# Attention with nine query steps per head instead of ten: the two short query chunks share one step

## The reference, cut to what matters

```
h = rmsnorm(x);  p = h @ w_in                      # uv | c_q | c_kv | k_rope | gate_a | gate_b
A = chunked gating of uv over 128-token chunks, @ w_a_out
q = rmsnorm(rmsnorm(c_q) @ w_uq)   per head: 8 heads, 128 plain + 64 rotary columns
k = rmsnorm(k_nope | k_rope),  v = 128 columns per head
o = softmax(q k^T * scale) @ v                     # bidirectional, within the group
B = o @ w_b_out
x = x + (sigmoid(gate_a) * A + sigmoid(gate_b) * B) @ w_out
x = x + expert-choice SwiGLU of rmsnorm(x): 16 experts, 2*n/16 tokens each
```

## Time and profile before

| what | value |
|---|---|
| median of three runs | 2089.08 us |
| lowest and highest of them | 2088.29 and 2089.18 us |
| span of the profiled execution, first to last instruction | 2087.1 us |
| instructions | 33261 |
| mean granted clock of TensorE | 0.994 |
| busy: TensorE, VectorE, ScalarE, GpSimd | 98%, 65%, 46%, 43% of the span |

### The profile page before, as it was taken

The page is one execution under the profiler, slowest core; times in us unless marked ns, Lnnn a source line. Parts: engine busy times, 40 slices in busy tenths (PEclk is TensorE's granted clock), DMA queues, the critical chain, the costliest instruction groups (busy, mean ns, idle before and its releaser), DMA issues.

```text
span 2087.1 us, 33261 instructions
## 1 busy us (share of the span) xinstructions
PE 2042.8 (98%) x13266; PEld 1683.2 (81%) x13266; DVE 1351.1 (65%) x1629; ACT 951.2 (46%) x1188; POOL 904.8 (43%) x640
## 2 busy tenths in 40 slices
PE   8999999999899999999999999899999999999997
PEld 8888888888789888888888887677777777777775
DVE  7864455456767477777754358876676667766774
ACT  8112211113555366666631032455556555555563
POOL 0975555566655376666642601412222222222221
PEclk9999999999999999999999999899999999999999
DMA  4223544324677622222134432688887778888873
GB/s 156 100 104 133 169 161 149 115 85 134 232 242 246 213 66 84 95 88 66 56 109 156 158 142 81 240 353 313 312 300 284 277 286 313 311 313 312 300 283 106
DMA packets 168938, 398.98 MB, mean 191 GB/s; under 512 B 16513, under 2 KB 88193, under 8 KB 168833
## 3 DMA queue, kind: packets, MB, share of 16 engines
q1 hardware_dynamic: 154096, 344.43, 45.0%
q0 software_dynamic: 7680, 20.98, 4.4%
q10 hardware_dynamic: 7056, 32.12, 4.4%
HBM read 318.19 MB, written 79.30 MB: 190 GB/s over the span
## 4 chain that ended last, share of the span: by engine, by line
PE 85%; DVE 8%; ACT 2%; POOL 2%; issue 1%; DMA 1%; SPq 0%; DVEq 0%; POOLq 0%; ACTq 0%
PE PS L1626 25%; PE PS L419 13%; PE PS L420 13%; PE PS L421 13%; PE PS L1657 8%; PE PS L1411 3%; PE PS L1398 1%; DVE topi L2663 1%; PE PS L1402 1%; PE PS L1399 1%; PE PS L1400 1%; PE PS L1401 1%; PE PS L1339 1%; DVE topv L2661 1%; DVE work L2665 1%
## 5 line engine op out<-in xcount | busy, mean ns | idle before, releaser
L419 PE MATMUL PS<-act_hi,w_hi 128*128 128x256 f32 (+1 forms) x800 | 275.2, 344 | 7.2 <-POOL w_lo L878 3.4
L420 PE MATMUL PS<-act_lo,w_hi 128*128 128x256 f32 (+1 forms) x800 | 270.1, 338 | 0.0
L421 PE MATMUL PS<-act_hi,w_lo 128*128 128x256 f32 (+1 forms) x800 | 269.7, 337 | 0.0
L981 POOL TENSOR_SCALAR prob<-prob,small 128x1024 f32<-128x1024 f32 (+1 forms) x80 | 200.6, 2508 | 120.7 <-DVE small L2551 120.7
L1051 POOL DMA_INDIRECT y_s<-ob_s,ixs_s x16 | 43.8, 2738 | 352.9 <-DVE ob_s L2822 352.9
L419 PEld LDWEIGHTS PS<-act_hi,w_hi 128*128 128x128 f32 x800 | 151.7, 190 | 24.8 <-POOL w_lo L878 3.7
L1626 PE MATMUL PS<-ehi,xT_hi 128*128 128x512 f32 x520 | 165.4, 399 | 0.6 <-DVE xT_lo L2736 0.4
L421 PEld LDWEIGHTS PS<-act_hi,w_lo 128*128 128x128 f32 x800 | 151.5, 189 | 16.3
L420 PEld LDWEIGHTS PS<-act_lo,w_hi 128*128 128x128 f32 x800 | 151.8, 190 | 14.8 <-issue 0.7
L1626 PE MATMUL PS<-elo,xT_hi 128*128 128x512 f32 x520 | 160.6, 390 | 0.0
L1626 PE MATMUL PS<-ehi,xT_lo 128*128 128x512 f32 x520 | 160.5, 390 | 0.0
(11 more groups left out here) (375 smaller groups left out, 5465.6 us busy)
## 6 DMA issues: line engine op xcount, KB each, us to landing
raw<-in_w_gate SPq DMA_DIRECT2D x64, 1024.0 KB, 8.8
raw_more<-in_w_up SPq DMA_DIRECT2D x32, 1024.0 KB, 12.6
raw_w<-in_w_up SPq DMA_DIRECT2D x32, 1024.0 KB, 16.6
w_raw<-in_w_in SPq DMA_DIRECT2D x16, 1024.0 KB, 7.7
w_raw<-in_w_down SPq DMA_DIRECT2D x15, 1024.0 KB, 5.7
stg<-in_w_down SPq DMA_DIRECT2D x15, 1024.0 KB, 7.8
gt<-in_w_down SPq DMA_DIRECT2D x15, 1024.0 KB, 13.0
raw_end<-in_w_down SPq DMA_DIRECT2D x15, 1024.0 KB, 14.9
```

The source lines that it names most:

```text
L419: pe.matmul(out, lh, rh, start=first, stop=False)
L420: pe.matmul(out, lh, rl, start=False, stop=False)
L421: return pe.matmul(out, ll, rh, start=False, stop=last)
L981: pool.tensor_scalar(prob[:, n % 3, 0:kn], prob[:, n % 3, 0:kn], prec[:, s:s + 1], None, ALU.mult).then_inc(S["norm_pool"], 1)
```

## The change

The two sample chunks of a head become one step, step 4 of nine, so there are 72 steps instead of 80. In the double step TensorE computes the scores of both chunks side by side in one bank, VectorE takes both maxima in one reduce and both biases in one operation, ScalarE still makes two exponentials, GpSimd multiplies both by their reciprocals with one operation whose second operand is broadcast. The four transposes go to one bank and are copied out in one operation on each engine, and the six value matmuls follow each other. The pairs of the prompt keep their halves.

The nine pieces of the next head are now turned in steps 1 to 8: none in step 0, one each in steps 1 to 5, pieces 5 and 6 in step 6, pieces 7 and 8 in steps 7 and 8. Piece 5 goes through bank 5, which the double step's transposes leave free, the others through bank 7; the transposes that follow in bank 5 wait for piece 5. SP loads the next tokens at a head's step 0, behind the store of the double step's values, under the same waits as before.

```diff
-ORD = (0, 1, 2, 3, 8, 9, 4, 5, 6, 7)
-STEPS = H * NCH
+TOKENS = ((0,), (1,), (2,), (3,), (8, 9), (4,), (5,), (6,), (7,))
+SH = len(TOKENS)
+STEPS = H * SH
+S_STEP = 4
...
+def turned_at(n):
+
+    h, s = divmod(n, SH)
+    first = PIECES * (h + 1)
+    return () if h == H - 1 else {0: (), S_STEP + 2: (first + 5, first + 6)}.get(s, (first + s - (s < S_STEP + 2),))
+
+
+def pair_of(n):
+
+    h, s = divmod(n, SH)
+    return 5 * h + (s // 2 if s < S_STEP else (s + 1) // 2)
+
+
+def half_of(n):
+
+    s = n % SH
+    return None if s == S_STEP else s % 2 if s < S_STEP else (s + 1) % 2
...
 def returns_at(n):
 
-    k = n - (STEPS - NCH + 2)
-    return {0: 0, 2: 1, 4: 2, 6: 3, 10: 4}.get(k)
+    k = n - (STEPS - SH + 2)
+    return {0: 0, 2: 1, 4: 2, 6: 3, 9: 4}.get(k)
...
         def x_bank(x):
-            return bank(6 + x % 2 if x < PIECES else 7)
+            if x < PIECES:
+                return bank(6 + x % 2)
+            return bank(5 if x % PIECES == 5 else 7)
...
             for n in range(STEPS + 4):
-                h, s = divmod(n, NCH)
-                if n % 2 == 0 and n >= 6:
-                    store_values((n - 6) // 2)
-                if h + 2 < H:
-                    if s == 9:
-                        sp.wait_ge(S["x_pe"], PIECES * (h + 1) + 9)
-                        load_queries(h + 2)
-                        sp.wait_ge(S["v_lo_pool"], h + 2)
-                        load_keys(h + 2)
-                if n == 2 * NCH:
+                h, s = divmod(n, SH)
+                if n >= 5 and half_of(n - 5) != 0:
+                    store_values(pair_of(n - 5))
+                if 0 < h < H - 1:
+                    if s == 0:
+                        sp.wait_ge(S["x_pe"], PIECES * h + 9)
+                        load_queries(h + 1)
+                        sp.wait_ge(S["v_lo_pool"], h + 1)
+                        load_keys(h + 1)
+                if n == 2 * SH:
...
                 pool.wait_ge(S["recip_dve"], n + 1)
-                pool.tensor_scalar(prob[:, n % 3, 0:kn], prob[:, n % 3, 0:kn], prec[:, s:s + 1], None,
-                                   ALU.mult).then_inc(S["norm_pool"], 1)
-                if s == 4 and h + 1 < H:
+                if s == S_STEP:
+                    both = prob[:, n % 3, 0:2 * TS].rearrange("p (c k) -> p c k", c=2)
+                    pool.tensor_tensor(both, both, prec[:, c:c + 2].unsqueeze(2).to_broadcast([P, 2, TS]),
+                                       ALU.mult).then_inc(S["norm_pool"], 1)
+                else:
+                    pool.tensor_scalar(prob[:, n % 3], prob[:, n % 3], prec[:, c:c + 1], None,
+                                       ALU.mult).then_inc(S["norm_pool"], 1)
+                if s == S_STEP and h + 1 < H:
                     split_values(h + 1)
...
-                free = x - 1 if h == 0 else x
+                free = x - 1 if h == 0 or i == 6 else x
...
-                q = slice(c * P, (c + 1) * P)
-                for o in range(0, kn, BANK):
-                    w = min(BANK, kn - o)
-                    out, k = bank(s_bank(n) + o // BANK, w), slice(k0 + o, k0 + o + w)
+                w = min(BANK, kn)
+                for c, o in [(c, o) for c in TOKENS[s] for o in range(0, kn, BANK)]:
+                    q, k = slice(c * P, (c + 1) * P), slice(k0 + o, k0 + o + w)
+                    first = s_bank(n) * BANK + o + c % 2 * w * (s == S_STEP)
+                    out = PS[:, first:first + w]
...
                 pe.wait_ge(S["norm_pool"], n + 1)
                 if n > 0:
                     pe.wait_ge(S["pt_lo_dve"], n)
+                if n % SH == S_STEP + 1 and n < STEPS - SH:
+                    pe.wait_ge(S["x_hi"], turned_at(n + 1)[0] + 1)
+                    pe.wait_ge(S["x_lo"], turned_at(n + 1)[0] + 1)
...
                 if n >= 4:
-                    values((n - 4) // 2, n % 2)
-                if h < H - 1 and s < PIECES:
-                    turn_head(PIECES * (h + 1) + s)
+                    values(n - 4)
+                if n < STEPS:
+                    for x in turned_at(n):
+                        turn_head(x)
...
-                act.activation(prob[:, n % 3, 0:kn], bank(s_bank(n), kn), ACT.Exp, bias=nmx[:, s:s + 1],
-                               scale=rq[:, h, c:c + 1], accum_out=psumr[:, s:s + 1]).then_inc(S["exp_act"], 1)
+                for c in TOKENS[s]:
+                    o = slice(c % 2 * kn, (c % 2 + 1) * kn) if s == S_STEP else slice(0, kn)
+                    last = act.activation(prob[:, n % 3, o], bank(s_bank(n), width(n))[:, o], ACT.Exp, bias=nmx[:, c:c + 1],
+                                          scale=rq[:, h, c:c + 1], accum_out=psumr[:, c:c + 1])
+                last.then_inc(S["exp_act"], 1)
...
-                if n == 0:
-                    high_head(PIECES)
                 if n < STEPS:
                     expo(n)
-                if n % 2 and 5 <= n:
-                    out_pair((n - 5) // 2)
-                if h < H - 1 and s < PIECES and n > 0:
-                    high_head(PIECES * (h + 1) + s)
+                if n >= 4 and half_of(n - 4) != 0:
+                    out_pair(pair_of(n - 4))
+                if n < STEPS:
+                    for x in turned_at(n):
+                        high_head(x)
...
-                dve.tensor_scalar(nmx[:, s:s + 1], mx[:, s:s + 1], rq[:, h, c:c + 1], -1.0, ALU.mult,
-                                  ALU.mult).then_inc(S["bias_dve"], 1)
+                dve.scalar_tensor_tensor(out=nmx[:, c:c + cn], in0=mx[:, c:c + cn], scalar=-1.0, in1=rq[:, h, c:c + cn],
+                                         op0=ALU.mult, op1=ALU.mult).then_inc(S["bias_dve"], 1)
```

More of the change, by code:

```diff
@@ L1381, in scores @@
             def scores(n):
-                h, s = divmod(n, NCH)
-                hd, c = heads[h % 2], ORD[s]
-                k0, kn = keys(c)
+                h, s = divmod(n, SH)
+                hd = heads[h % 2]
+                k0, kn = keys(TOKENS[s][0])
                 if s == 0:
@@ L1405, in turn_prob @@
             def turn_prob(n):
-                kn = keys(ORD[n % NCH])[1]
+                kn = width(n)
                 pe.wait_ge(S["norm_pool"], n + 1)
@@ L1409, in turn_prob, with values @@
                     pe.wait_ge(S["pt_lo_dve"], n)
+                if n % SH == S_STEP + 1 and n < STEPS - SH:
+                    pe.wait_ge(S["x_hi"], turned_at(n + 1)[0] + 1)
+                    pe.wait_ge(S["x_lo"], turned_at(n + 1)[0] + 1)
                 for k in range(kn // P):
-                    last = pe.transpose(bank(4, kn)[:, k * P:(k + 1) * P], prob[:, n % 3, k * P:(k + 1) * P], ident[:])
+                    o = (0, 2, 1, 3)[k] if n % SH == S_STEP else k
+                    last = pe.transpose(bank(4, kn)[:, o * P:(o + 1) * P], prob[:, n % 3, k * P:(k + 1) * P], ident[:])
                 last.then_inc(S["probT_pe"], 1)
-            def values(pr, half):
+            def values(n):
+                pr, half = pair_of(n), half_of(n)
                 h = pr // 5
                 hd = heads[h % 2]
-                k0, kn = keys(ORD[2 * (pr % 5)])
-                ks = kn // P // 2
-                if half == 0:
-                    pe.wait_ge(S["pt_lo_dve"], 2 * pr + 2)
+                k0, kn = keys(first_of(pr))
+                ks = kn // P
+                if half != 1:
+                    pe.wait_ge(S["pt_lo_dve"], n + 1 if half is None else n + 2)
                     if pr % 5 == 0:
@@ L1424, in values @@
                         pe.wait_ge(S["values_act"], pr)
-                for k in range(half * ks, (half + 1) * ks):
+                for k in range(ks) if half is None else range(half * ks // 2, (half + 1) * ks // 2):
                     v = slice(k0 + k * P, k0 + (k + 1) * P)
                     last = mm3(pe, bank(6, 2 * P), hd["v_hi"][:, v], hd["v_lo"][:, v], pt_hi[:, pr % 2, k],
-                               pt_lo[:, pr % 2, k], k == 0, k == 2 * ks - 1)
-                if half:
+                               pt_lo[:, pr % 2, k], k == 0, k == ks - 1)
+                if half != 0:
                     last.then_inc(S["values_pe"], 1)
@@ L2034, in high @@
             def high(n):
[L2035 to L2037 removed]
                 act.wait_ge(S["probT_pe"], n + 1)
[L2039 to L2042 removed]
+                if half_of(n) != 1 and pair_of(n) > 1:
+                    act.wait_ge(S["values_pe"], pair_of(n) - 1)
+                act.activation(turned_part(pt_hi, n), turned_bank(n), ACT.Copy).then_inc(S["pt_hi_act"], 1)
             def expo(n):
[L2045 to L2047 removed]
+                h, s = divmod(n, SH)
+                kn = keys(TOKENS[s][0])[1]
                 act.wait_ge(S["bias_dve"], n + 1)
@@ L2563, in _ @@
                     low(n - 2)
-                if n == 0:
-                    low_head(PIECES)
                 if n < STEPS:
                     inverse(n)
-                if h < H - 1 and s < PIECES and n > 0:
-                    low_head(PIECES * (h + 1) + s)
```

(2 more changed lines are left out.)

49 lines of the change are left out of this document (23 added, 26 removed).

## The result

The changed kernel takes 2130.79 us (median of four runs, 2128.46 to 2131.39) against 2089.13 us: ratio 1.020, 95% interval 1.0187 to 1.0212. It is 41.7 us slower. The forecast was 2102.0 with a range of 2096 to 2115, so the sign was right and the size short by 28.8 us. The profiled execution has a span of 2128.8 us and a mean granted clock of 0.985.

The account below looks back on a forecast made before the run. TensorE, busy 98% of the span, was taken as the bound. Heads 1 to 6 +12.0, head 0 +1.5, head 7 -2.3 and clock +1.7 gave +12.9 on 2089.1: 2102.0 us, range 2095.8 to 2115.

Parts of the forecast that it names:

- TensorE's own work of a head: Nine steps of a head's matmuls and transposes on TensorE: 42.41 us against 43.51, if nothing new waits.
- the gap: TensorE idles before the next head's first scores, waiting for the last piece: 3.1 us, seven times, 21.7 us.
- The loads of the next head: SP's load of the next tokens, issued about 2 us later, was called covered before its first piece: 0.
- the gap is hidden: Rival: the last piece's chain ends before TensorE reaches the next head's scores, so the kernel gets faster, 2078.6 us; 8%.
- what would show it: Signs: seven TensorE idles of about 3 us released by VectorE's L2501, heads of about 45.5 us, head 7 near 39.2.
- I take one such fall among seven gaps, +1.7: Granted clock behind TensorE's idle stretches before a head's scores: one drop to mostly 1.2 GHz, costing 1.7 us.
- the clock falls behind every gap: Rival: the clock drops after all seven idle stretches before a head's scores, 11.9 us instead of 1.7, 2112.2 us; 17%.
- The walk of step 7: Delays counted from the start of step 6: step 7's exponential at 9.28 us, ahead of step 8's start at 9.86.
- The bias in its new form reads a column more: nothing beside 0.21: VectorE's bias operation with its extra column read was taken to add nothing to its 0.21 us.
- 0.9 of slack: Bank 5: piece 5's low part done about 6.3 us, step 7's transposes start at 7.20, so no wait.
- the microsecond that I allowed: Head 0: 40.7 us against 39.27, +1.5, trusted to 1 us.
- The pile-up rival: ScalarE and VectorE lose another 0.6 us in step 6; TensorE's idle becomes 3.7 us, 4.2 more, 2106.2 us; 10%.

Follow-up runs that it names:

- experiment 10: Changed kernel with old bias form for single chunks, own buffer for the double step, last piece in step 7, piece kinds reordered: 2077.41 us, ratio 0.995.
- experiment 3: Changed kernel with the single-chunk bias in its old form and own buffers for the double step's turned probabilities: 2108.87 us, ratio 1.0096.
- experiment 6: Changed kernel with the last piece back in step 7, two pieces in step 6, none in step 8, loads at step 8: 2090.86 us, ratio 1.0012.
- experiment 11: The kernel of experiment 10 without the double step's own buffers: 2081.83 us, ratio 0.9969.
- experiment 12: The kernel of experiment 10 without the own buffers and with the changed kernel's two-tensor-input bias in all steps: 2093.40 us, ratio 1.0024.
- experiment 7: Changed kernel with a head's last piece copied out ahead of the last step's exponential and reciprocal: 2123.16 us, one execution.
- experiment 8: The kernel of experiment 3 with the last piece ahead of exponential and reciprocal, but behind the low half of step 6: 2103.19 us, ratio 1.0069.
- experiment 1: Changed kernel with the single-chunk bias in its old form, the double step keeping the new one: 2126.58 us, ratio 1.018.
- experiment 2: Changed kernel with own buffers for the double step's turned probabilities: 2121.13 us, ratio 1.016.
- experiment 4: Changed kernel with GpSimd splitting the next head's values one step later: 2127.43 us, one execution.

## Why the prediction was right in sign and wrong in size

**What held.** TensorE's own work of a head was right to 0.04 us (42.41; 42.44 in experiment 10), so was the place of the gap, the order that makes it and its length once the two unforeseen waits are gone (3.09 us by pitch, measured 3.19 in experiment 3). GpSimd's broadcast multiply took 1.04 us where I took 1.10. The loads of the next head cost nothing in the changed kernel (they did in experiments 6, 11 and 12, where less time lies between their issue and the first piece). The rival "the gap is hidden" had the price 2078.6; the version that hides it measured 2077.4, though that near match has luck in it, since 1.8 us of its gain lie ahead of attention. In heads 1 to 6 of the changed kernel steps 1 to 5 are each within 0.02 us of the working. Of "what would show it", the gaps' releaser held in substance: the view names ScalarE's L2068 six times of seven, but L2552, as L2501 is called now, ends 0.05 us behind it (807.46 against 807.41) and 0.10 ahead of the scores. Head 7 took 41.3 instead of 39.2, 1.65 of it for the fall in its first step.

**The steps that failed**, with their share of the missing 28.8 us:

- *The clock: "I take one such fall among seven gaps, +1.7".* There were seven, and they cost 15.0 us, 2.1 each: +13.3. I reasoned from the one gap shown, 3.39, that a shorter one would mostly be spared. Experiment 3, whose gap is the 3.1 that I foretold, has six of seven falls; so this step was wrong by itself, not only because the gap came out longer. The rival "the clock falls behind every gap", at 17%, was the true course, and its price of 1.7 us was right in experiment 3 (gaps of 2.98), low in experiment 7 (gaps of 3.02, 1.9 in the mean) and lower still for the longer ones of the change. The Trainium skill's section (TensorE: Matmul & The Clock Gate, HAM oscillation), named in the prediction, has a kernel that comes back at half clock after each wait; the changed kernel's seven windows agree. Those of experiments 3 and 8 do not: one of seven and four of seven show 1.00.
- *The walk of step 7: "exponential 9.28".* I let ScalarE's high copy be free to run and looked at banks and semaphores of the pieces, but not at which pair had the buffer of the turned probabilities. Merging the two sample chunks gives the double step a buffer for itself, and the next pair's copy lands on values not yet done. The exponential is 1.5 us later against step 8, and step 8 idles 4.6 instead of 3.1: 7 x 1.5 = +10.5. Experiments 1 and 2 show that it is this wait and not the bias that sets the gap while both are there. Taking away the wait alone gave back 0.9 of the 1.5; the other 0.5 to 0.6 came back only with the old bias on top (experiment 3), so that share of the 10.5 has both causes.
- *"The bias in its new form reads a column more: nothing beside 0.21".* It takes 0.16 when free, but 2.30 once per head. With it, *"0.9 of slack"* for piece 5 fell: its low part ended 1.3 later, at 7.6 instead of 6.3. Steps 6 and 7 take 0.11 and 0.47 us more, 7 x 0.58 = +4.1; taking it away gave 4.2.
- The rest, 28.8 - 13.3 - 10.5 - 4.1 = 0.9, is in head 0 and head 7, within the microsecond that I allowed.

The pile-up rival (gap 3.7) had the right length for another reason: the double piece itself loses nothing, since in experiment 3 the walk through it holds to 0.1 us.

## What to carry to other kernels

When an order written out by hand gets shorter, redo the rotation of every buffer and every bank, not only of those that the edit names: two buffers that fitted ten steps made a wait in nine. A dependency at the end of a period needs a cover as long as its whole chain; here the step without a piece was that cover, and 40 of 41.7 us came back by putting it at the end of the head again. And an idle stretch of TensorE has to be priced with the clock behind it: at gaps of 3 us the fall came nearly every time and added half to the price.

## What the runs showed of the hardware

- A one-column VectorE operation with two tensor inputs in SBUF (L2590) took 2.30 us when it started inside GpSimd's `v_lo` (L1017), and 1.17 us inside `v_hi` (L1015), and ended within 0.02 us of it in all fourteen cases of the two kernels. In its old form, one tensor and a column as scalar operand, it never took longer than 0.22, also the seven times that it started inside `v_lo` in experiment 1. Operations with one input in PSUM were not held: the seven maxima that started inside `v_hi` (785.93) took their usual 1.22 or 1.23, and in experiment 4 the seven two-chunk low parts that started inside `v_lo` (793.61) 0.48 or 0.49. The Trainium skill (SBUF — State Buffer, SBUF: two separate sides) has VectorE operations with two SBUF inputs and GpSimd operations lock the pair of ports that they share for a whole instruction; the two kernels agree for the split of the values. They do not for GpSimd's multiply by a column (L1030): thirty biases of the changed kernel fall inside it and take 0.16, and only one takes 0.36. The multiply itself is not free of VectorE: it took 4.0 us instead of 2.85 the three times in head 7 that it started 0.2 us behind a VectorE subtraction of two SBUF tensors of 1280 columns (`o_hl`, 1.47 us; one of them from 1077.54, the multiply from 1077.72), and the 0.36 fell into one of these. What makes that operation different was not tried.
- Whether the granted clock falls behind a stop of TensorE is not settled by the stop's length alone: behind 2.38 us it fell three times of seven, behind 2.98 six of seven, though the heads of one kernel are alike. Behind 1.40 it never did, behind 3.0 and more (28 + 7 + 7 gaps) always. A fall cost 1.7 us at gaps of 2.38 and 2.98, and anything from 1.4 to 3.0 us at gaps of 3.02 to 3.75 (the longest is the step 0 from 1005.78, 7.57 instead of 4.60).
